# Conformer and gMLP trunk on one core: where the diagonal tap matrices are made, and the order of some scalings

## What is computed

```
def conformer_conv_module(x, w_in, b_in, w_dw, b_dw, ln_g, ln_b, w_out, b_out):
    h = x @ w_in + b_in
    a, gate = jnp.split(h, 2, axis=-1)
    h = a * jax.nn.sigmoid(gate)
    h = causal_depthwise_conv(h, w_dw, b_dw)          # 31 taps, each channel by itself
    h = jax.nn.silu(layer_norm(h, ln_g, ln_b))
    return h @ w_out + b_out
...
x = layer_norm(DEEPNORM_ALPHA * x + y, norm1_g[i], norm1_b[i])
y = conv_ffn(x, ...)                                  # up, 3-tap conv, silu gate, down
x = layer_norm(DEEPNORM_ALPHA * x + y, norm2_g[i], norm2_b[i])
```

## Time and profile before

| what | value |
|---|---|
| median of 3 runs | 1052.95 us (1051.62 to 1053.39) |
| the profiled execution's own time | 1052.61 us |
| its span in the profile | 1050.9 us |
| busy: PE, PEld, DVE | 1032.8 us (98%), 860.1 (82%), 805.9 (77%) |
| busy: ACT, POOL | 505.6 us (48%), 235.4 (22%) |
| shares of the chain that ended last | PE 87%, DVE 6%, POOL 2%, ACT 2% |

### The profile page before, as it was taken

How to read it: one execution, slowest core, us unless ns; L and a number is a source line. 1 busy time by engine, 2 the same in 40 slices (tenths; PEclk the granted TensorE clock), 3 DMA queues, 4 the chain that set the end, 5 groups by cost and what they waited for, 6 DMA issues and landing times.

```text
span 1050.9 us, 14219 instructions
## 1 busy us (share of the span) xinstructions
PE 1032.8 (98%) x4803; PEld 860.1 (82%) x4803; DVE 805.9 (77%) x1145; ACT 505.6 (48%) x741; POOL 235.4 (22%) x269
## 2 busy tenths in 40 slices
PE   9999989999999999999999999999999999999996
PEld 7788778988888888888888888898888888888885
DVE  7899985688677676788885786669767676779887
ACT  6899935344334343366553442334434333346643
POOL 4989820323432000000010120042334100000002
PEclk9999999999999999999999999999999999999999
DMA  9587417799989222286555422779999723237652
GB/s 346 158 192 167 119 36 254 217 232 257 252 254 206 88 99 101 80 279 202 198 182 181 140 101 98 271 174 275 246 220 244 194 81 118 80 100 266 200 195 100
DMA packets 64859, 189.17 MB, mean 180 GB/s; under 512 B 7472, under 2 KB 8496, under 8 KB 64816
## 3 DMA queue, kind: packets, MB, share of 16 engines
q1 hardware_dynamic: 44144, 137.76, 38.0%
q0 software_dynamic: 18656, 43.53, 21.5%
q10 hardware_dynamic: 2016, 7.34, 2.1%
HBM read 178.11 MB, written 54.53 MB: 221 GB/s over the span
## 4 chain that ended last, share of the span: by engine, by line
PE 87%; DVE 6%; POOL 2%; ACT 2%; issue 1%; DMA 1%; SPq 1%; DVEq 0%; POOLq 0%; ACTq 0%
PE ps L1378 18%; PE ps L1379 18%; PE ps L1380 18%; PE ps L1580 5%; PE ps L1582 5%; PE ps L1581 5%; PE ps L1388 4%; PE ps L1390 4%; PE ps L1389 4%; POOL gsum L510 1%; PE ps L1531 1%; DMA par<-d_params 1%; DVE wl L919 1%; DVE res L1192 1%; PE ps L1469 1%
## 5 line engine op out<-in xcount | busy, mean ns | idle before, releaser
L1378 PE MATMUL ps<-xh,wh 128*128 128x512 f32 x816 | 317.7, 389 | 0.3 <-DVE wl L919 0.3
L1379 PE MATMUL ps<-xl,wh 128*128 128x512 f32 x816 | 317.5, 389 | 0.0
L1380 PE MATMUL ps<-xh,wl 128*128 128x512 f32 x816 | 317.5, 389 | 0.0
L1378 PEld LDWEIGHTS ps<-xh,wh 128*128 128x128 f32 x816 | 153.2, 188 | 32.6 <-DVE wl L919 0.7
L1380 PEld LDWEIGHTS ps<-xh,wl 128*128 128x128 f32 x816 | 153.2, 188 | 31.9
L1379 PEld LDWEIGHTS ps<-xl,wh 128*128 128x128 f32 x816 | 153.2, 188 | 31.8
L609 ACT ACTIVATE wh<-raw 128x1024 fp32r<-128x1024 f32 x118 | 124.2, 1057 | 95.1 <-PE ps L1582 63.4
L919 DVE TENSOR_TENSOR wl<-raw,wh 128x1024 fp32r<-128x1024 f32 x106 | 128.9, 1221 | 46.4 <-ACT wh L609 46.3
L488 POOL TENSOR_SCALAR veps<-sqs 128x1 f32<-128x1 f32 x16 | 7.9, 492 | 573.7 <-ACT squares L739 573.7
L1580 PE MATMUL ps<-wh,parts 128*128 128x512 f32 x264 | 103.1, 391 | 0.2
L1581 PE MATMUL ps<-wl,parts 128*128 128x512 f32 x264 | 102.7, 389 | 0.0
(11 more groups left out here) (166 smaller groups left out, 1696.9 us busy)
## 6 DMA issues: line engine op xcount, KB each, us to landing
raw<-d_weights SPq DMA_DIRECT2D x156, 512.0 KB, 4.3
raw<-summed SPq DMA_DIRECT2D x56, 512.0 KB, 3.7
summed<-d_weights POOLq DMA_DIRECT2D x88, 256.0 KB, 8.1
summed<-d_weights SPq DMA_DIRECT2D x66, 256.0 KB, 6.5
summed<-summed POOLq DMA_DIRECT2D x46, 256.0 KB, 5.6
wl<-raw POOLq DMA_DIRECT2D x12, 512.0 KB, 6.8
xraw<-d_x_fm SPq DMA_DIRECT2D x8, 256.0 KB, 5.5
res<-d_x_tm SPq DMA_DIRECT2D x4, 512.0 KB, 7.4
```

The lines of the kernel that those rows point to most:

```text
L1378: eng.matmul(ps[:, bank, cols], a, xh[:, k, cols], start=(k == 0), stop=False)
L1379: eng.matmul(ps[:, bank, cols], a, xl[:, k, cols], start=False, stop=False)
L1380: mm = eng.matmul(ps[:, bank, cols], b, xh[:, k, cols], start=False, stop=(k == KD - 1))
```

## The change

`POOL_TILES` goes from 2 to 7. So POOL makes all the diagonal matrices of tiles 0 to 6, and ACT none but seven pairs of tile 7. POOL's order is new: it makes those of tile 1 amid the additions of tile 0, those of tile j + 1 after the fourth addition of tile j, and the nine of tile 7 after the additions of tile 1. In `taps` PE's wait counts accordingly.

Three other pieces move. ACT scales `brow` behind the first products of tile 1, not ahead of `gluh`. DVE makes the low part `glul` of tile 1 ahead of its taps k = 0 and 1. In `ffn_down`, for n = 1 the low part of block 1 (`block_lo`) comes ahead of `normed` of block 2; for n = 3 `normed` of block 1 comes after the sum of block 2, and `normed` of block 2 ahead of the sum of block 3.

```diff
-POOL_TILES = 2
+POOL_TILES = 7
...
-        for j in range(POOL_TILES):
-            diagonals(j, 0, PE_TAPS[j])
-        diagonals(KD - 1, PE_TAPS[KD - 3], PE_TAPS[KD - 3] + POOL_LAST)
-        add_products(0, range(1, GP_TAPS[0]))
+        diagonals(0, 0, PE_TAPS[0])
+        add_products(0, range(1, AT_ONCE))
+        diagonals(1, 0, PE_TAPS[1])
+        add_products(0, range(AT_ONCE, GP_TAPS[0]))
         for j in range(1, KD):
             for u in (2 * j + LEAD, 2 * j + 1 + LEAD):
                 if u in BY_DMA:
                     lo(u)
-            add_products(j, range(1, GP_TAPS[j]))
+            add_products(j, range(1, AT_ONCE))
+            if 1 < j + 1 < POOL_TILES:
+                eng.wait_ge(dw_pe, j)
+                diagonals(j + 1, 0, PE_TAPS[j + 1])
+            add_products(j, range(AT_ONCE, GP_TAPS[j]))
...
+            if j == 1:
+                diagonals(KD - 1, PE_TAPS[KD - 3], PE_TAPS[KD - 3] + POOL_LAST)
...
-            if j == 1:
-                eng.wait_ge(bo1_in, 16)
-                eng.activation(brow[:, :], brow[:, :], ACT.Copy, scale=1.0 / ALPHA).then_inc(bo1_ok, 1)
...
             if j == 0:
                 his([1 + LEAD])
+            if j == 1:
+                eng.wait_ge(bo1_in, 16)
+                eng.activation(brow[:, :], brow[:, :], ACT.Copy, scale=1.0 / ALPHA).then_inc(bo1_ok, 1)
...
-                if k == 2 and j < KD - 1:
+                if k == (0 if j == 1 else 2) and j < KD - 1:
                     gated_low(j)
...
-            normed(n, 1)
             if n < 3:
+                normed(n, 1)
...
+            if n == 3:
+                normed(n, 1)
             centred(n, 2)
             if n < 3:
                 los([U_GV + 3])
-                normed(n, 2)
+                block_lo(n, 1)
+            normed(n, 2)
             eng.wait_ge(w_used, u0 + DOWN)
             add(3, 0, p4 + 1, 1.0, True)
             eng.wait_ge(c_rd, read + R_P4 + 2)
             mean_of(n, 3)
-            if n < 3:
-                block_lo(n, 1)
-            else:
-                normed(n, 2)
             centred(n, 3)
...
-                eng.wait_ge(diag_p, j + 1)
+                eng.wait_ge(diag_p, j + 1 if j <= 2 else j + 2)
```

## The result

| | before | changed kernel |
|---|---|---|
| median time | 1052.97 us (1051.16 to 1054.41, 10 runs) | 1054.89 us (1054.27 to 1056.29, 10 runs) |
| ratio to before | | 1.0022, 95% interval 1.0014 to 1.0031 |
| profiled execution: time, span | 1052.61, 1050.9 us | 1055.33, 1053.6 us |

The changed kernel is 1.9 us slower, 0.18% by the two medians and 0.22% by the ratio of the runs. The prediction said 1056 with a range of 1052.5 to 1059, and gave slower by over 0.2% a chance of 0.65.

The account below looks back on a forecast made before the run. The prediction took PE as 98% busy and POOL as full in the convolution. It summed 4.25 - 0.8 - 0.2 = +3.2 us onto 1052.61, giving 1055.9, set at 1056 because the median was 0.3 higher; range 1052.5 to 1059.

Parts of the forecast that it names:

- POOL is full and the selects come out at DVE's sum: Convolution: POOL works 14.42 of 14.83 us a tile, so added selects delay DVE's sum of tile 5 by 5.7 us.
- a pair of five: POOL, tiles 1 to 5: each added pair of five-matrix selects costs 1.41 us, 7.05 us for five tiles.
- the nine-matrix pair: POOL, moved behind tile 1's additions: adds 2.8 us to the chain, ends 2.3 and 3.4.
- POOL's start: POOL, tile 0: additions begin sooner, so POOL is 0.55 us earlier, at 35.5 instead of 36.05; ends 35.3 and 37.2.
- POOL's tile with the pair: POOL, convolution: a tile with added selects takes 15.83 us, against the 14.83 at which PE and DVE go.
- the loss is mostly swallowed: Rival: cheaper selects or low-end terms, and 0.95 gained at the end, leave +0.3 to +2 us, 1053 to 1055; chance 0.18.
- the signs: Expected in the trace: POOL's tile 15.8 us, DVE waiting 1 to 3 us and PE about 1 us each tile.
- The sigmoid wait of 1.45: DVE, tile 6: its 1.45 us wait for ACT's sigmoid falls away, cutting the 5.7 us lateness to 4.25.
- fall at unit 15: Rival: PE stands some 1.8 us before unit 15, its clock falls, +1.6 us, 1057.6; chance 0.2.
- I count zero: Moving `brow` and tile 1's `glul`: PE gains up to 3.4 us there, nothing of it left at tile 5.
- is worth nothing more: ACT loses 50 activations, some 14.7 us; this gives only the 2.7 us of POOL's idle time already counted.
- The two small moves: `ffn_down`: earlier `block_lo` of block 1 gains 0.8 us, the new order at the end 0.2 net.

Follow-up runs that it names:

- e5: The changed kernel with POOL_TILES at 4 instead of 7; median 1053.89 us, ratio to before 1.0010.
- e7: The changed kernel with POOL_TILES at 2 and POOL waiting for `glul` of tile 1 before its additions there; median 1051.36 us, ratio to before 0.9993.
- e8: The changed kernel with POOL_TILES 2, eleven matrices of tile 7 made amid tile 6's additions, POOL waiting for `glul` in tiles 1 and 2; 1050.25 us.
- e10: e8 without POOL's wait for `glul` in tile 2, keeping the one in tile 1; median 1049.44 us, ratio to before 0.9965.
- e11: e10 with POOL's remaining wait for `glul` in tile 1 taken out; median 1050.27 us, ratio to before 0.9980.
- e1: The kernel before with only the new order in `ffn_down` (n = 1 and n = 3); median 1052.46 us, ratio to before 0.9997.
- e9: e8 with nine instead of eleven matrices of tile 7 on POOL; median 1051.85 us, ratio to before 0.9997.
- e2: The changed kernel with POOL_TILES back at 2, all else kept; median 1052.01 us, ratio to before 0.9994.

## Why the prediction was right, and where its numbers were not

**That POOL is full and the selects come out at DVE's sum** was right, and the doubled selects show it. In the changed kernel POOL's end of tile 5 is 115.49 - 17.40 = 98.09 us after the first select, against 110.18 - 16.31 = 93.87 before: 4.2 us late, and not the 6.6 (116.8 - 110.18) of the sum. Its terms:

| term | taken | measured |
|---|---|---|
| a pair of five | 1.41 | 94.45 - 93.03 = 1.42 |
| the nine-matrix pair | 2.8 | 54.09 - 51.77 = 2.32 |
| POOL's start (from the first select) | -0.55 | (36.38 - 17.40) - (36.05 - 16.31) = -0.76 |
| POOL's tile with the pair | 14.42 + 1.41 = 15.83 | 100.00 - 84.53 = 15.47 |

**The mis-sized step** is POOL's tile of 15.83 us, "14.42 + 1.41". The net 0.36 us a tile over five tiles is 1.8 us; with 0.5 for the nine-matrix pair and 0.2 for the start that is 2.5, and POOL was 2.4 us less late. Both of its terms were too large:

- The pair costs its tile less than its own 1.42 us. From the start of an addition it is 1.44 us to the next addition, which waits for the one before it (`gp_add`), but 1.24 to a select, which does not. So a pair amid the additions costs 1.42 - 0.20 = 1.22. Its place on the engine was counted in full, what it frees was not. This is 1.0 of the 1.8 us.
- A tile without pair and wait is shorter than 14.42. In e5 the two `lo` DMAs and eight additions last 81.87 - 68.21 = 13.66 us (13.68 and 13.69 in e7 and e8), where the sum had 2.06 + 11.77 = 13.83: 0.16 less, 0.8 us in five tiles. It is not that the DMAs hide under the additions. In the changed kernel the first addition starts at 86.40, while the DMA row from 85.11 still runs to 87.18, so 0.77 us of the row is overlapped; but that addition takes 2.25 us to the next in place of 1.44, 0.81 more, which takes the 0.77 back. What is shorter is the second addition: before, `glul` held it (1.74 us at 70.16, 0.44 more than the 1.30 of the others), and with the earlier start it is held less (1.56 at 88.65).

I had bounded the selects by their own rows and not by what surrounds them. The start came out near by two errors that cancel: DVE's subtraction for unit 4 made one of tile 0's additions 2.19 us long before (at 28.16), which the 12.2 us had in them, and now holds a select instead, so that the pair for tile 1 takes 30.83 - 28.40 = 2.43 and the additions 11.1. The nine-matrix pair had a low end of 2.3 in the prediction, from its own row; taking the 2.8, which included the distance to the first addition, was the wrong choice.

**Luck and signs.** The nine-matrix pair (2.3) and the start (-0.2) both came out at the low ends that the rival "the loss is mostly swallowed" had asked for, so a part of that rival came true inside the forecast. The upper ends of the forecast's own range add up to +4.5, that is 1060.4 and not 1059. Of the signs, POOL's additions without a wait for ACT in tiles 1 to 5 and the missing wait at 555 are there. A tile lasts 15.5 and not 15.8 us. DVE waits for `gsum` by 0.28 to 0.58 us in tiles 3 to 5, and not by 1 to 3 in each, and PE waits for `glul` by 0.89, 2.67 and 0.33 us in three tiles, not by 1 us in each.

**From POOL's lateness to the end.** DVE's sum of tile 5 comes at 115.67 - 17.40 = 98.27 against 111.18 - 16.31 = 94.87: 3.40 late (predicted 5.7). The sigmoid wait of 1.45 falls away, as predicted: 1.95. Then `glul` of tile 6 took 1.46 us in place of 0.68, 0.78 that the prediction did not have: 2.73, which is 127.70 - 124.97. Predicted were 4.25.

**The unforeseen mechanism** is the held `glul`. What counts is where it falls against an addition of POOL. Before, POOL's first addition of a tile started after a wait for ACT, whose product comes from the same `glu` as `glul` does: 68.72 and `glul` at 70.07, 1.35 us later, in the gap between two additions, and 0.68 long; POOL's second addition stood behind it. Without that wait the first addition starts when POOL is ready, and `glul` falls into it: in tile 1 it comes 38.60 - 37.76 = 0.84 us after the addition's start and takes 1.63, in tile 2 it comes 55.48 - 55.21 = 0.27 us after and takes 2.52. In tile 6 it falls into the second addition (118.73) at 119.09. POOL's lost pause was also what kept the two apart. The Trainium skill ("SBUF — State Buffer", section on who interferes with whom) says that a DVE instruction with two SBUF inputs and a POOL instruction reading SBUF exclude each other for a whole instruction; the prediction used this only to price the selects. The traces agree with it here: 0.68 in a gap, 1.33 to 2.52 in an addition, 0.94 where the addition had 0.4 us to go (88.12). Curing it in tile 1 gave 0.93 us (e10 against e11). In tiles 2 and 6 no run cured it alone; that it cost the changed kernel 0.78 in tile 6 rests on the account above.

**Clock.** The rival had its fall at unit 15, behind a wait of 1.8 us. The wait was 0.73, since POOL was less late, and the clock stayed at 1.00. It fell in tile 2 instead, after a wait of 2.67, and in e5, after 2.64 at the same place, it did not. A fall is thus a matter of the single execution, and what one costs in the convolution is small here: e1, whose convolution is that of before, has its fall at 41 to 44 us and none behind tile 7, and its stretch is within 0.1 us of before's. "I count zero" for `brow` and `glul` of tile 1 fits: POOL's rate decided what stood at tile 5. That those two moves alone would have been worth something is not shown; no kernel had them alone.

**ACT's relief "is worth nothing more"** was right for tiles 1 to 5: what POOL waited for ACT fell from 4.3 us to 2.3, of which 2.0 is the wait for the first product of tile 0, and no more came of it. The relief where ACT is the last, in tiles 6 and 7, took 1.2 us out of DVE's wait for two pairs (e8 against e9), and the change left those seven pairs with ACT.

**The two small moves** were right. From the transposes of tile 7 to PE's last matmul it takes 899.95 us against 900.77 before, -0.82 (predicted -0.8); from there to the last `normed` 4.40 against 4.68, -0.28 (predicted -0.2). The last row of `veps` takes 0.19 us in place of 1.14, and the obstacle returns one block earlier, at 1043.03, as foreseen, which delays the last sum. Together -1.10, the same within 0.1 in the seven kernels e2 to e9, and -1.0 in e1.

Sum: 2.73 - 1.10 = +1.63 us by the traces, +1.92 by the medians, +3.2 predicted. The difference of 0.3 between traces and medians is within the spread of either kernel's runs; it is the same way round as in every experiment, and its cause is open.

## What to carry to other kernels

Before work is put on an engine, take its free time from its row of work in that stage, and not from its share of the span (POOL's was 22% here, with 0.4 us free in 14.8). Take the distances from one start to the next, with what stands before and behind: an addition was 1.44 us to another addition and 1.24 to a select, and one that began under a DMA row gave back in its length what it had gained in its start. An engine that loses its pauses also starts to meet instructions that it never met before, so look at which two-input DVE instruction stands where the pause was; and work is worth moving off an engine only where something waits for that engine (two pairs in tile 7 took 1.2 us out of a wait; 50 activations in tiles 2 to 6 gave only the pauses of POOL, which its new work used up).

## What the runs showed of the hardware that was not expected

- POOL goes on to its next instruction while the row of the DMA that it issued last still runs: two `lo` DMAs are a row of 2.07 us, and the addition behind them starts 1.29 us after its start. The first addition then lasts longer (2.11 us at 86.40 and 2.23 at 55.21, where one is 1.29 when nothing is beside it), so that little is won, and the `glul` that fell into the one at 55.21 took 2.52 us.
- Two instructions of two engines can keep out of each other's way for a whole stage because one wait fixes their distance (1.35 us, as in the earlier trace rows), without anything in the program that says so.
- A pair of selects takes POOL 1.42 us for five matrices and 2.32 for nine, 0.28 and 0.26 us a pair of matrices, with ends that overlap the next instruction's start; amid additions the five cost 1.22.
- The length of one wait of PE does not tell whether its clock falls. Behind 2.67 us (changed kernel, tile 2) and 3.00 us (e10 and e11, tile 7) it was at half at once; behind 2.64 us (e5, tile 2) it stayed full, and behind 3.02 us (e8, tile 7) it fell a microsecond later. Behind the 2.27 us at tile 7 it fell within 2 us in before and in the changed kernel, and not in e2, e5 and e7.
- What a fall costs hangs on its place: the rest is 904.27 to 904.43 us with or without one that comes a microsecond or two after the transposes of tile 7 begin, and 905.29 and 905.30 with one that comes before them. In e10 that took back 1.0 of 3.3 us.
